# Expert stages of a two-block transformer: half of the token gather issued after the first expert's products, row parts in their own buffers, router block by block

## The reference

```python
probs_g = softmax(xf @ w_group + b_group)             # 4 groups, top 1
p_top, g_idx = top_k(probs_g, 1)
in_group = take_along_axis(logits_e, g_idx)           # 4 experts of that group
w_top, e_local = top_k(softmax(in_group), 2)          # top 2 inside it
gates = einsum(p_top * w_top, one_hot(ids, 16))
h = silu(einsum('td,edf->tef', xf, w_gate)) * einsum('td,edf->tef', xf, w_up)
y = einsum('tef,efd->td', h * gates, w_down)          # 16 experts, width 256
x = layer_norm(ALPHA * x + y)
```

## Time and profile before

| what | value |
|---|---|
| median of 3 runs | 1449.96 us (1448.72 to 1451.22) |
| the profiled execution's own time | 1453.92 us |
| its span | 1452.3 us |
| mean granted clock of PE | 0.967 |
| PE busy | 1368.9 us, 94% |
| DVE busy | 1037.6 us, 71% |
| ACT busy | 767.6 us, 53% |
| POOL busy | 88.4 us, 6% |
| HBM read | 325.56 MB |

### The profile page before, as it was taken

The page is one execution under the profiler, slowest core; times in us unless marked ns, Lnnn a source line. Parts: engine busy times, 40 slices in busy tenths (PEclk is TensorE's granted clock), DMA queues, the critical chain, the costliest instruction groups (busy, mean ns, idle before and its releaser), DMA issues.

```text
span 1452.3 us, 19475 instructions
## 1 busy us (share of the span) xinstructions
PE 1368.9 (94%) x7482; PEld 1172.9 (81%) x7482; DVE 1037.6 (71%) x1057; ACT 767.6 (53%) x753; POOL 88.4 (6%) x81
## 2 busy tenths in 40 slices
PE   5989999999899999999999988999998988999995
PEld 5977878888799778888999977888878977788884
DVE  7768768888676565445575757788886465888886
ACT  2666434343434443443464445777774565577773
POOL 0000001010000000000000013100004000400000
PEclk9999899999999999999999997999998999999998
DMA  9967569997675375555543342999993423499990
GB/s 359 388 236 244 188 215 306 300 311 263 209 261 176 103 261 174 183 194 173 175 142 120 116 132 86 317 335 349 348 356 123 150 66 104 130 347 349 350 351 36
DMA packets 208909, 327.72 MB, mean 226 GB/s; under 512 B 9456, under 2 KB 146352, under 8 KB 208832
## 3 DMA queue, kind: packets, MB, share of 16 engines
q1 hardware_dynamic: 195536, 276.71, 56.4%
q0 software_dynamic: 13296, 49.93, 10.2%
HBM read 325.56 MB, written 1.05 MB: 225 GB/s over the span
## 4 chain that ended last, share of the span: by engine, by line
PE 80%; DVE 11%; ACT 5%; DMA 2%; issue 1%; SPq 0%; DVEq 0%; ACTq 0%; POOLq 0%
PE ps L2159 23%; PE ps L2161 22%; PE ps L2160 22%; DVE w_low L1369 3%; ACT w_high L687 2%; PE ps L2684 1%; PE ps L2882 1%; PE ps L2788 1%; DMA scratch<-in_w_ada 1%; PE ps L2526 1%; DMA raw<-in_w_qkv 1%; DVE stats L1880 1%; DVE h_low L2034 1%; DVE x_rows L1871 1%; PE ps L2245 1%
## 5 line engine op out<-in xcount | busy, mean ns | idle before, releaser
L1369 DVE TENSOR_TENSOR w_low<-raw,w_high 128x2048 fp32r<-128x2048 f32 x254 | 588.3, 2320 | 273.2 <-ACT w_high L687 271.1
L687 ACT ACTIVATE w_high<-raw 128x2048 fp32r<-128x2048 f32 x254 | 484.4, 1908 | 344.8 <-PE ps L2161 317.2
L2159 PE MATMUL ps<-w_high,h_high 128*128 128x512 f32 (+1 forms) x888 | 352.4, 397 | 8.7 <-DVE h_low L1464 3.9
L2161 PE MATMUL ps<-w_high,h_low 128*128 128x512 f32 (+1 forms) x888 | 345.2, 389 | 0.0
L2160 PE MATMUL ps<-w_low,h_high 128*128 128x512 f32 (+1 forms) x888 | 345.1, 389 | 0.0
L2159 PEld LDWEIGHTS ps<-w_high,h_high 128*128 128x128 f32 x888 | 168.6, 190 | 43.8 <-issue 8.1
L2161 PEld LDWEIGHTS ps<-w_high,h_low 128*128 128x128 f32 x888 | 168.4, 190 | 34.7
L2160 PEld LDWEIGHTS ps<-w_low,h_high 128*128 128x128 f32 x888 | 168.6, 190 | 32.0 <-issue 0.2
L2159 PE MATMUL ps<-h_high,w_high 128*128 128x256 f32 x592 | 174.9, 295 | 4.2 <-DVE h_low L1464 4.2
L2160 PE MATMUL ps<-h_low,w_high 128*128 128x256 f32 x592 | 170.7, 288 | 0.0
L2161 PE MATMUL ps<-h_high,w_low 128*128 128x256 f32 x592 | 170.6, 288 | 0.0
(11 more groups left out here) (367 smaller groups left out, 1481.9 us busy)
## 6 DMA issues: line engine op xcount, KB each, us to landing
raw<-in_w_down SPq DMA_DIRECT2D x124, 512.0 KB, 4.8
raw<-in_w_gate_up SPq DMA_DIRECT2D x88, 512.0 KB, 5.1
scratch<-in_w_ada POOLq DMA_DIRECT2D x40, 1024.0 KB, 5.5
raw<-in_w_gate SPq DMA_DIRECT2D x80, 512.0 KB, 5.0
raw<-in_w_up SPq DMA_DIRECT2D x80, 512.0 KB, 6.2
raw<-in_w_qkv SPq DMA_DIRECT2D x24, 512.0 KB, 13.2
raw<-in_w_o SPq DMA_DIRECT2D x24, 512.0 KB, 4.7
raw<-in_w_in SPq DMA_DIRECT2D x24, 512.0 KB, 4.9
```

Of the source, the lines that this page charges most:

```text
L687: act.activation(wh[u % SPL][:, :, 0:w], raw[u % RAW][:, :, 0:w], ACT.Copy).then_inc(h_split, 1)
L1369: dve.tensor_tensor(wl[u % SPL][:, :, 0:w], raw[u % RAW][:, :, 0:w], wh[u % SPL][:, :, 0:w].bitcast(F32), ALU.subtract).then_inc(l_split, 1)
L2159: pe.matmul(o, h1, h2, start=start, stop=False, skip_group_check=True)
L2161: return pe.matmul(o, l1, h2, start=False, stop=stop, skip_group_check=True)
```

## The change

The edits below are made for both expert stages, as both run through the same functions.

1. The row parts get buffers of their own: the high part lies in the buffer `rows` (`tv`), the low part half in the features and half in scratch. ACT no longer waits for `router_sums` ahead of L1157. DVE makes the low part in two halves, and makes it after the last small operation of the group search (L1945), ahead of the places and the selections.
2. The gather is made in two halves by window: windows 0 and 1 where it was (32 products of 256 columns), windows 2 and 3 after `gate_up(0)` (another 32 of 256 columns, ahead of the first `turn()`). ACT evicts each in eight operations of 256 columns; the second eight stand after the first tile's `silu`.
3. Unit 4's split moves on ACT and DVE from behind `product(0)` to behind the first `high` and `low_part`.
4. `sel_turn` waits for the second eight evictions.
5. The router goes block by block, both halves of tokens for each block.
6. Dummy products: 14 instead of 10 ahead of the transposes, 3 new ones between the two halves' transposes (in `after_norm`, so also at the third call of it), 11 instead of 8 ahead of the router, 5 new ones ahead of the wait for the groups.

GpSimd's program has no edit: its products still wait for both parts of window 0.

```diff
@@ ACT: sort_in and the tile loop
+                def windows_out(w0, k):
+                    if k % 2 == 0:
+                        act.wait_ge(gathered, gth.up())
+                    act.activation(in_windows[:, w0:w0 + 2, k, :], gather_bank(k).rearrange("p (w s) -> p w s", w=2),
+                                   ACT.Identity, bias=shift[:, k:k + 1], scale=scale[:, k:k + 1]).then_inc(gather_taken, 1)
+                    gtk.up()
                 def sort_in():
-                    act.wait_ge(router_sums, rsum.up())
                     act.activation(rows_h, x_parts, ACT.Copy).then_inc(rows_high, 1)
...
                     for k in range(KT):
-                        act.wait_ge(gathered, gth.up())
-                        act.activation(in_windows[:, 0:GRP, k, :], ps[:, GBANK[k], :]...
+                        windows_out(0, k)
...
                 split()
                 silu()
-                split(1, True)
+                for k in range(KT):
+                    windows_out(2, k)
                 n[0] += 2
                 for c in range(1, NTILE):
                     high()
+                    if c == 1:
+                        split(-1, True)
                     split()
@@ DVE: sort_in and the tile loop
+                dve.wait_ge(rows_high, rhi.up())
+                for i, x in enumerate(rows_l):
+                    ks = slice(UK * i, UK * i + UK)
+                    dve.tensor_tensor(x, x_parts[:, ks, :, :], rows_h[:, ks, :, :].bitcast(F32), ALU.subtract).then_inc(rows_low, 1)
+                    dve.wait_ge(rows_low, rlo.up())
                 place, over = by_tile(rt[:, 304:312]), rt[:, 312:314]
...
-                dve.wait_ge(rows_high, rhi.up())
-                dve.tensor_tensor(rows_l, x_parts, rows_h.bitcast(F32), ALU.subtract).then_inc(rows_low, 1)
-                dve.wait_ge(rows_low, rlo.up())
...
                 product(0)
-                split(1)
                 n[0] += 2
                 for c in range(1, NTILE):
                     low_part()
+                    if c == 1:
+                        split(-1)
                     split()
@@ PE
+                    if t == 0:
+                        keep_busy(3, 0)
             def router():
-                keep_busy(8, 0)
+                keep_busy(11, 0)
-                for t in range(TT):
-                    for k in range(KT):
-                        bank_of_h(t == 0, k)
+                for k in range(KT):
+                    bank_of_h(True, k)
+                    for t in range(TT):
                         pe.matmul(ps[:, 3, 40 * t:40 * t + 40], hh[:, k, tok], rwr[:, k, :], ...)
                         i = pe.matmul(ps[:, 3, 40 * t:40 * t + 20], hl[:, k, tok], rwh[:, k, :], ...)
...
+                    keep_busy(5, 0)
                     pe.wait_ge(group_ready, grp.up())
...
+                def gather(k, w0, low):
+                    part = rows_l[k // UK][:, k % UK] if low else rows_h[:, k]
+                    for t in range(TT):
+                        i = pe.matmul(gather_bank(k), part[:, t, :], sel_r[t][:, w0 * P:(w0 + 2) * P], ...)
+                    if low and k % 2:
+                        i.then_inc(gathered, 1)
+                def other_windows():
+                    pe.wait_ge(gather_taken, gtk.up(KT))
+                    for k in range(0, KT, 2):
+                        for low in (False, True):
+                            for j in range(2):
+                                gather(k + j, 2, low)
                 def sel_turn():
+                    pe.wait_ge(gather_taken, gtk.up(KT))
...
                 gate_up(0)
+                other_windows()
...
-            after_norm(5, 10)
+            after_norm(5, 14)
-            after_norm(7, 10)
+            after_norm(7, 14)
```

More of the change, by code:

```diff
@@ L121, in build @@
         tv = sb("rows", [P, TT, D])
+        rows_at = nc.sbuf_base - TT * D * 4
+        rows_hi = nc.alloc_sbuf_tensor_at("rows_high_part", [P, KT, S], F32R, offset=rows_at)
         W = sb("scratch", [P, 41 * 256])
+        scratch_at = nc.sbuf_base - 41 * 256 * 4
+        rows_lo = [nc.alloc_sbuf_tensor_at(f"rows_low_part{i}", [P, UK, S], F32R, offset=o)
+                   for i, o in enumerate((features_at + 16 * S * 4, scratch_at + 20 * 256 * 4))]
         Z = sb("small", [P, 8 * 256])
@@ L161, in build @@
         rt = W[:, 12 * 256:20 * 256]
-        rows_h, rows_l = (a[:, :, :].rearrange("p k (t s) -> p k t s", t=TT) for a in (hh, hl))
+        rows_h = rows_hi[:, :, :].rearrange("p k (t s) -> p k t s", t=TT)
+        rows_l = [a[:, :, :].rearrange("p k (t s) -> p k t s", t=TT) for a in rows_lo]
         x_parts = xs[:, :, :].rearrange("p t (k s) -> p k t s", s=P)
@@ L2779, in sort_in @@
                     pe.wait_ge(rows_high, rhi.up())
-                    for k0 in (0, 4):
-                        for part in (rows_h, rows_l):
-                            if part is rows_l and k0 == 0:
+                    for k0 in (0, UK):
+                        for low in (False, True):
+                            if low:
                                 pe.wait_ge(rows_low, rlo.up())
-                            for k in range(k0, k0 + 4):
-                                if part is rows_h and k >= 6:
-                                    pe.wait_ge(gather_taken, gtk.value(k - 3))
-                                for t in range(TT):
-                                    i = pe.matmul(ps[:, GBANK[k], :], part[:, k, t, :], sel_r[t],
-                                                  start=part is rows_h and t == 0, stop=part is rows_l and t == 1, skip_group_check=True)
-                                if part is rows_l:
-                                    i.then_inc(gathered, 1)
-                                    gth.up()
-                    gtk.up(8)
+                            for k in range(k0, k0 + UK):
+                                gather(k, 0, low)
+                def gather(k, w0, low):
+                    part = rows_l[k // UK][:, k % UK] if low else rows_h[:, k]
+                    for t in range(TT):
+                        i = pe.matmul(gather_bank(k), part[:, t, :], sel_r[t][:, w0 * P:(w0 + 2) * P],
+                                      start=not low and t == 0 and k % 2 == 0, stop=low and t == 1, skip_group_check=True)
+                    if low and k % 2:
+                        i.then_inc(gathered, 1)
+                        gth.up()
+                def other_windows():
+                    pe.wait_ge(gather_taken, gtk.up(KT))
+                    for k in range(0, KT, 2):
+                        for low in (False, True):
+                            for j in range(2):
+                                gather(k + j, 2, low)
                 def gate_in():
```

12 lines of the change are left out of this document (5 added, 7 removed).

## The result

| | before | after |
|---|---|---|
| median, both in one comparison | 1450.43 us (1448.72 to 1453.51, 6 runs) | 1443.74 us (1442.58 to 1445.32, 6 runs) |
| ratio, 95% interval | | 0.9949 (0.9939 to 0.9960) |
| profiled execution, own time | 1453.92 us | 1443.61 us |
| its span | 1452.3 us | 1441.9 us |
| PE busy | 1368.9 us | 1365.9 us |

The account below looks back on a forecast made before the run. PE was taken to bound the expert tiles, leaving gains at the stages' entries: 5.1 and 3.1 us, together 8.2, less 1.0 behind them, gives 7.2 off 1449.96, so 1442.8 us. Its own range was 1440.8 to 1444.5, the wider one 1440.8 to 1449.5.

Parts of the forecast that it names:

- PE bounds, the stream doesn't: Expert stages: PE's products bound the tiles; the weight queue waits only for DVE. Rival of the stream bounding: 1450.4 us, 0.10.
- Router, R earlier by 2.6 and 1.1: Stage entries: DVE begins the group search 2.6 us earlier in the first stage, 1.1 in the second.
- Place 4.1 and 4.6 behind R: DVE's places (L1951) start 4.1 and 4.6 us behind the group search's start, losing 0.2 and 0.7.
- Place to W shorter by 2.3 + 0.4: From DVE's places to window 0 having both parts: low row part out, 2.3 us; ACT wait gone, 0.4, each stage.
- W to T, 19.2 for 18.7: From window 0 ready to PE's first product behind the second turn: 0.5 us longer per stage; first turn at 9.0.
- unit 4 at W + 15.3: Weights of down(0): DVE's split, taken as 2.9 us, ends 15.3 us after window 0 is ready; PE stands 0.4.
- fits neither cleanly: DVE's 3.42 us split beside GpSimd's 4.21 us products was said not to match the exclusive-lock rule of whole-instruction waits cleanly.
- The edits that cost nothing: Dummy products ahead of and between the transposes fill PE's waits, and sel_turn's wait ends in time: no cost.
- The sum: Whole kernel: 8.2 us gained up to window 0 ready, less 1.0 behind it, 7.2 us off: 1442.8 us.
- The new hole: Rival: PE waits 2.6 us ahead of gate_up(0), which then starts slow, losing 1.65 per stage; 1446.1 us, chance 0.25.
- Unit 4 late: Rival: down(0)'s weights really late in both stages, second turn's end 2.8 us later than before; 1447.4 us, chance 0.12.
- The slow clock by halving: Rival: 256-column gather products keep PE at 1.2 GHz, 9.1 us per stage; 11.0 slower, 1461 us, chance 0.08.

Follow-up runs that it names:

- no dummies: The changed kernel without any of the added dummy products: median 1447.94 us, 0.9975 of the kernel before.
- gates spread: Changed kernel, gates' 20 small products spread among gate_up(0)'s second unit's groups, reading the other buffer half, so not computing the same: 1443.35 us, ratio to before 0.9941.
- rows late: The changed kernel with the low row part put back behind the selections, its own buffers kept: median 1452.13 us, 0.9998 of the kernel before.
- all three: Changed kernel, unit 4 split in old order, gates' small products spread (other buffer half read), nine dummies for four ahead of the gather: 1443.58 us, ratio to before 0.9947.
- unit 4 old, gates later: Changed kernel, unit 4 split in its old order, gates' small products moved behind both units of gate_up(0): 1441.43 us, ratio to before 0.9931.

## Why the prediction was right, step by step

- **PE bounds, the stream doesn't.** Held: PE is busy 95% of the span, and the load queue waits for splits alone (DVE's, and 0.4 us for ACT's).
- **Router, R earlier by 2.6 and 1.1.** Measured 2.68 and 1.21, with DVE's weight split right ahead of R in both stages, as said.
- **Place 4.1 and 4.6 behind R.** Measured 4.24 and 5.00; in the second stage DVE stood 0.79 us for the counts, at a clock of 0.50. In `no dummies` it is 4.24 there, also at 0.50; in the changed kernel profiled again it is 4.24 with the five added dummy products, as the clock was back at 1.00 in time. So the 0.8 takes both, the dummy products and the low clock, as the prediction had it.
- **Place to W shorter by 2.3 + 0.4.** Measured 2.7 and 2.9. The sum was right, and its reason was half the story: it takes the halved gather as well, else the gather becomes the bound (2.2 to 3.5 us). W: forecast 5.1 and 3.1 earlier, measured 5.0 and 3.0.
- **W to T, 19.2 for 18.7.** This step failed in both terms. I put the first turn at W + 9.0 "at a clock of 1.00". At full clock that is right (9.0 in ten of the twenty stages profiled with the gather in halves and the low part early), but in the changed kernel the clock fell in `gate_up(0)` in both stages, 1.5 us each. And unit 4 at W + 15.3 came at W + 16.0 at full clock (`gates spread`, first stage): ACT was on time (its split ended at W + 12.3, forecast 12.4), DVE's split took 3.64 and not 2.9 us. PE stands 1.25 us and not 0.4. The reading that 3.42 us beside products of 4.21 "fits neither cleanly" was wrong, too: record by record these are full waits (last section). The two don't add, one covers the other, and W to T is 20.4 in both stages: 1.7 us lost in each, not 0.5. The "0.5 later" was 1.2 too small, twice.
- **"The edits that cost nothing."** This failed too, to the good side. I priced the dummy products as costs and never as a gain, and looked at two norms of three. The run without the third norm's says 2.1 us, the one without any 4.2. The profiled pair has 2.7 us between the third norm and the second stage, of which 1.1 come where no edit lies.
- **The sum.** In the profiled pair 5.0 + 3.0 - 3.3 + 2.7 = 7.4, which is their 10.3 less the 2.9 ahead of the stages; forecast 7.2. The total is right because two misses of 2.4 and 2.7 us cancel, and a part of the second is the execution's and not the change's. The mechanism up to W was right; that the total came out is luck.
- **The rivals.** The new hole came in half. In the first stage of the changed kernel the hole ahead of `gate_up(0)` is 0.25 us, as most of the gather ran at 1.2 GHz; in the second it is 1.37 us. Yet the clock falls in both, 5 to 6 us behind it, and costs 1.5 of the 1.65 us that the rival named. In `rows late` the hole is there as described, and a fall right behind it. Unit 4 late came half true. The slow clock by halving did not come as told: the first half's products do start 0.21 us apart at first, behind PE's wait of 2.13 us, but the clock is back before they end, the second half's start 0.12 us apart, and so do the first half's in `all three`.

The parts taken out one by one cost 8.3 (row part), 3.3 (halves), 4.7 (router order) and 4.2 us (dummies): 20.5 in all, for a change of 7 to 8. They don't add. That each fills a hole which lets the others' time pass at the full clock is my reading, and not shown.

## What to carry to other kernels

A hole in PE's work is priced with the clock behind it: 2.5 us on DVE's chain, 1.2 and 1.3 us net at W, cost 2.7 and 3.8 us by the second turn here (`rows late`). Before calling a dummy product free, look up every caller of the function that it is put in, and price what it may gain as well as what it costs. A split moved to just in time needs the duration that it has beside its real neighbour, and the deadline at the full clock: a slow stretch ahead of it can hide that it is late. And one profile is one execution: before a gain between two landmarks is put down to an edit, the kernel without that edit should lack it.

## What the runs showed of the hardware that I had not expected

- **The clock falls with PE busy.** In the changed kernel the granted clock goes from 1.00 to 0.50 at about 891, more than 5 us after PE's last idle time, of 0.25 us. Two executions of the same kernel differ in it in the same stage (second: W to first turn 10.6 and 9.0). Where it fell like this, a row of 20 small products had ended at most 1.1 us before.
- **A 2.4 us hole, both ways.** Behind it the clock held once and fell once in the same execution of `all three`; behind 3.54 and 4.64 us (`rows late`) it fell.
- **DVE and GpSimd wait for each other's whole instructions.** In `gates spread` the product lasts 2.40 us, as it does alone, and ends at 902.78; the split starts 1.49 us earlier and takes 3.64, its own 2.28 and 1.36 more. In `unit 4 old, gates later` (second stage) the same pair is 2.41 and 3.66, with 1.51 us of overlap. The Trainium skill, "SBUF — State Buffer", section "Who interferes with whom", says just this: the loser waits for the rest of the other instruction. Here the trace agrees, and at this place the prediction should have followed it. It agrees for splits and products in a row, too, once they are read one by one. The two splits of 6.68 us in the earlier trace rows are these (kernel before; DVE, then GpSimd's second product):

```profile
896.14 2.28 DVE L1369 TENSOR_TENSOR w_low<-raw,w_high 128x2048 fp32r<-128x2048 f32 x1
898.35 4.48 DVE L1369 TENSOR_TENSOR w_low<-raw,w_high 128x2048 fp32r<-128x2048 f32 x1
```

```profile
900.76 4.29 POOL L656 TENSOR_TENSOR x_rows<-x_rows,scratch 128x1024 f32<-128x1024 f32 x1
```

The first split is under way when the first product starts (896.47) and lasts its own 2.28. The product waits for its end and takes 4.21 instead of 2.40. The second split starts 2.33 us before that product ends and takes 2.20 more than its own; the second product starts 2.07 us before that split ends and takes 1.89 more. By turns each waits for the rest of the other; none is slowed in proportion.
